# Head preparation under the input projection, a regrouped order of the modulation sums and fillers, and a second expert-choice layer on 32 live rows with nine landing places

## What is computed

```python
# first block
h = rms_norm(x, attn_norm_g);  proj = h @ w_in              # 1024 -> 3688 columns
dq, dk, dv, iq, ik, iw, cq, ckv, kpe, gd, gm = split(proj)  # 512 64 64 512 64 8 256 128 32 1024 1024
q_a, k_a = rope(rms_norm(dq heads)), rope(rms_norm(dk))     # 9 heads of 64: "qk"
q_i, k_i = rope(iq heads), rope(ik)                         # 9 heads of 64: "ix"
score = sum_h relu(q_i . k_i) * iw ; keep the top 64 keys of each query
out_a = attention(q_a, k_a, dv, only the kept keys)
q_b, kv_b = rms_norm(cq) @ mla_w_uq, rms_norm(ckv) @ mla_w_ukv   # then head norm, rope, causal attention
x += (sigmoid(gd) * (out_a @ w_br_dsa) + sigmoid(gm) * (out_b @ w_br_mla)) @ w_out
x += memory_cross_attention(...);  x += hierarchical_moe(...)    # 16 experts, 2 of a group
# second block: two layers, each modulated by m = silu(c) @ ada_w + ada_b  (6 x 1024 columns)
x += g1 * ssd_mixer(...)        # layer 0;   layer 1: attention over latent and context tokens
x += g2 * moe_ec(...)           # both layers, expert choice:
def moe_ec(h, router_w, w1, w3, w2):
    cap = 2 * T // 16                                # 32 tokens for each of 16 experts
    gate, idx = top_k(softmax(h @ router_w).T, cap)
    xg = h[idx]
    y = (silu(xg @ w1) * (xg @ w3)) @ w2 * gate      # w1, w3, w2: 1024 x 1024 each
    return zeros.at[idx].add(y)
return rmsnorm(x, final_norm_w)
```

## Time and profile before

| | us |
|---|---|
| median of 3 runs | 2287.35 (2286.69 to 2291.01) |
| the profiled execution | 2282.53 |
| its span, first to last instruction | 2280.7 |
| TensorE busy | 2077.5 (91%) |
| VectorE busy | 955.1 (42%) |
| ScalarE busy | 637.1 (28%) |
| filler products, 212 records | 104.0 |
| weights of both expert-choice layers | 427 GB/s in most slices from 1140 on |

### The profile page before, as it was taken

One profiled execution on the slowest core, in us unless ns is written; L12 is line 12 of the kernel. 1 busy time (PEld: TensorE's weight loads), 2 busy tenths in 40 slices (PEclk: granted clock), 3 DMA queues, 4 the chain that ended last, 5 costly groups with the idle time before them and its releaser, 6 DMA issues. The chain is left out here.

```text
span 2280.7 us, 25273 instructions
## 1 busy us (share of the span) xinstructions
PE 2077.5 (91%) x10338; PEld 1120.2 (49%) x10338; DVE 955.1 (42%) x1595; ACT 637.1 (28%) x1264; POOL 69.5 (3%) x95
## 2 busy tenths in 40 slices
PE   6978898899999999999999998988898899988887
PEld 5744444444467888888643333322445433332222
DVE  4375523545588988893432222222357400000001
ACT  4222312211257766772221111100117110100000
POOL 0001000000000000000000000000020000000000
PEclk9989998999999999999999999999999999999999
DMA  8656156899623333332389999999820399999996
GB/s 307 214 216 235 42 183 252 345 390 387 241 77 93 112 111 130 111 111 73 130 343 428 427 428 428 427 427 428 323 99 1 148 416 426 426 426 427 427 427 293
DMA packets 145705, 623.59 MB, mean 273 GB/s; under 512 B 14995, under 2 KB 65686, under 8 KB 108598
## 3 DMA queue, kind: packets, MB, share of 16 engines
q1 hardware_dynamic: 140672, 601.65, 66.1%
q0 software_dynamic: 2352, 16.91, 1.9%
q10 hardware_dynamic: 2566, 3.41, 0.5%
HBM read 620.76 MB, written 1.18 MB: 273 GB/s over the span
## 5 line engine op out<-in xcount | busy, mean ns | idle before, releaser
L2798 PE MATMUL bank<-slots,xgTe 128*64 128x512 f32 x1648 | 370.9, 596 | 44.0 <-DMA slots<-in_moe_w 44.0
L2798 PEld LDWEIGHTS bank<-slots,xgTe 128*64 128x64 f32 x1648 | 116.4, 137 | 276.0 <-issue 215.0
L3007 DVE TENSOR_TENSOR actse<-sge,bank 128x512 f32<-128x512 f32 x32 | 22.0, 688 | 529.1 <-PE bank L2798 529.1
L2798 PE MATMUL bank<-slots,aTe 128*64 128x512 f32 x832 | 189.6, 597 | 19.1 <-issue 19.1
L511 PE MATMUL bank<-slots_r 128*128 128x512 f32 x512 | 200.0, 391 | 0.0
L2911 ACT ACTIVATE sge<-bank 128x512 f32<-128x512 f32 x32 | 19.1, 597 | 485.2 <-PE bank L2798 485.2
L510 PE MATMUL bank<-hT_r,slots_r 128*128 128x512 f32 x384 | 154.0, 401 | 0.0
L512 PE MATMUL bank<-slots_r 128*128 128x512 f32 x384 | 150.3, 391 | 0.0
L574 PE MATMUL bank<-slots,hT 128*128 128x512 f32 (+1 forms) x320 | 131.5, 572 | 1.6 <-DVE hT L551 0.7
L2798 PEld LDWEIGHTS bank<-slots,aTe 128*64 128x64 f32 x832 | 61.1, 136 | 126.7 <-issue 126.7
L506 PE MATMUL bank<-consts 128*128 128x512 f32 x212 | 104.0, 644 | 7.7 <-PEq L1954 3.4
(11 more groups left out here) (536 smaller groups left out, 3116.8 us busy)
## 6 DMA issues: line engine op xcount, KB each, us to landing
slots<-in_moe_w SPq DMA_DIRECT2D x155, 2048.0 KB, 29.5
extra0e<-in_moe_w SPq DMA_DIRECT2D x25, 2048.0 KB, 29.5
slots<-in_ada_w SPq DMA_DIRECT2D x24, 2048.0 KB, 10.1
slots<-in_ssd_in_w SPq DMA_DIRECT2D x48, 512.0 KB, 5.3
slots<-in_moe_w_gate SPq DMA_DIRECT2D x23, 1024.0 KB, 10.6
slots<-in_moe_w_up SPq DMA_DIRECT2D x23, 1024.0 KB, 12.6
slots<-in_moe_w_down SPq DMA_DIRECT2D x23, 1024.0 KB, 7.5
rowsB<-acum_rows POOLq DMA_DIRECT2D x16, 1024.0 KB, 5.8
```

Of the source, the lines that this page charges most:

```text
L2798: i = pe.matmul(bank[64 * n:64 * n + 64, :], lhsT(4 * h + k), wv[:, 0, n * 512:(n + 1) * 512], start=(h == 0 and k == 0), stop=(h == 1 and ...
L3007: dve.tensor_tensor(acts[:, :], sg[:, :], psum[1][:, :], ALU.mult).then_inc(a_ready, 1)
```

## The change

It has six parts. (1) rope of ix, the sum, the scale and rope of qk are issued by VectorE inside the input projection, after the splits of the chunks 3 to 6, with scratch space in the buffer C. (2) The c norm of MLA (squares, roots, scales) moves to the front of DSA; DSA keeps one ada group, which comes after the relevances, and its VectorE part stands in round 4 of the top-k. (3) MLA has both its ada groups after its products; a new group, `mix_ada`, is put in the merge block. The list of weight pieces follows that order. (4) Fillers: 106 become 45. (5) In the second expert-choice layer the padding is gone: 32 columns in `xgT`, and silu, gate and scale work on the two live groups of 32 partitions, in two instructions each; `acts` is set to zero once. (6) That layer's ring has nine places; the ninth is extra2 with columns 2048 to 4095 of hT, free once `quarters` has been computed.

```diff
@@ stream of weights
         ada_weights()
+        weights("mla", [...])
         ada_weights()
-        ada_weights()
-        weights("mla", [...])
         ada_weights()
         weights("br_dsa", ...); weights("br_mla", ...)
+        ada_weights()
...
-        moe2_weights(1, (4, 5, 0, 1, 2, 3, SLOTS + 1, SLOTS + 2))
+        moe2_weights(1, (4, 5, 0, 1, 2, 3, SLOTS + 1, SLOTS + 2, SLOTS + 3))
@@ input projection, VectorE, after split_in(dve, n + 2, ...)
+                    if n == 3:
...
+                        rope(dve, link, ix, ix, tmp, 9, 32, 64, 0, cos(32), sin(32))
+                    if n == 4:
+                        hnorm.vector_sum(dve, link, qk, sq, 9, 64)
+                    if n == 5:
...
+                        hnorm.vector_scale(dve, link, qk, qk, [...], 9, 64)
+                    if n == 6:
+                        rope(dve, link, qk, qk, tmp, 9, 32, 64, 0, cos(32), sin(32))
@@ DSA, TensorE
-                ada0.tensor(pe)
-                pe.wait_ge(ix_ready, 1)
                 to_ixT.tensor(pe)
...
-                ada1.tensor(pe)
-                pe.wait_ge(qk_ready, 1)
+                ada0.tensor(pe)
                 to_qkT.tensor(pe)
-                hold(pe, 6)
                 to_qkT.wait_all(pe)
@@ DSA, VectorE, in the top-k
+                    if r == 4:
+                        ada0.vector(dve)
@@ MLA, TensorE
-                ada0.tensor(pe)
                 pe.wait_ge(c_normed, 1)
                 to_cT.tensor(pe)
...
+                ada0.tensor(pe)
                 ada1.tensor(pe)
-                hold(pe, 17)
                 pe.wait_ge(heads_ready, 1)
@@ merge
+                mix_ada.tensor(pe)
                 pe.wait_ge(merged_ready, 4)
                 to_mT.tensor(pe)
@@ memory block, SSD, attention
-                hold(pe, 3)
...
-                        hold(pe, 9, pair[0].ap)
+                        hold(pe, 8, pair[0].ap)
...
-                hold(pe, 5)
                 norm.tensor(pe)
-                hold(pe, 13)
...
-                hold(pe, 10)
+                hold(pe, 9)
@@ expert choice
-                    hold(pe, 7 if l == 0 else 4)
+                    if l == 1:
+                        hold(pe, 4)
                     norm.tensor(pe)
-                    hold(pe, 3 if l == 0 else 1)
...
+                    extra_room[2].freed = (bank_full, b.full)     # behind quarters
...
-                                    i = pe.matmul(bank[64 * n:64 * n + 64, :], lhsT(4 * h + k), ...
+                                    i = pe.matmul(bank[64 * n:64 * n + NJ * CAP, :], lhsT(4 * h + k), ...
...
+                LIVE = [slice(0, P)] if NJ == 2 else [slice(0, CAP), slice(64, 64 + CAP)]
...
-                        dve.memset(xgT[:, :, :, :, CAP:2 * CAP], 0.0)
+                        link(dve.memset(acts[:, :], 0.0))
...
-                        dve.tensor_tensor(acts[:, :], sg[:, :], psum[1][:, :], ALU.mult).then_inc(a_ready, 1)
+                        for r_ in LIVE:
+                            i = dve.tensor_tensor(acts[r_, :], sg[r_, :], psum[1][r_, :], ALU.mult)
+                        i.then_inc(a_ready, 1)
```

More of the change, by code:

```diff
@@ L212, in build @@
         banks = Banks(psum, emptied)
-        slot_loaded = [sem(f"slot_loaded{i}") for i in range(SLOTS + 3)]
+        slot_loaded = [sem(f"slot_loaded{i}") for i in range(SLOTS + 4)]
         ring = Ring(slots, slot_loaded)
@@ L262, in build @@
         ada_weights()
+        weights("mla", [(0, 2, 768, rows("mla_w_uq")), (1536, 1, 1024, rows("mla_w_ukv"))])
         ada_weights()
-        ada_weights()
-        weights("mla", [(0, 2, 768, rows("mla_w_uq")), (1536, 1, 1024, rows("mla_w_ukv"))])
         ada_weights()
@@ L317, in build @@
         w_v = [A[f"moe_w{m}_2"].rearrange("l e (h p j) n -> p (l e) h (j n)", h=2, j=4) for m in (1, 3, 2)]
-        extra_room = [Piece(None, None, 0, None) for _ in range(2)]
+        extra_room = [Piece(None, None, 0, None) for _ in range(3)]
         ring.last[SLOTS] = extra_room[0]
@@ L335, in build @@
         ring.last[SLOTS + 1] = ring.last[SLOTS + 2] = extra_room[1]
+        ring.last[SLOTS + 3] = extra_room[2]
         for n in (0, 1, 2):
@@ L910, in tensor @@
                         back(c - 1)
-                hold(pe, self.held)
                 back(self.pieces[-1])
@@ L1156, in _ @@
             def _(pool):
-                hnorm.pool(pool, 9, 64)
+                pool.wait_ge(c_squared, 4)
+                root(pool, 0, 2, MLA_QR)
+                root(pool, 2, 2, MLA_KVR, c_rooted)
             @block.scalar
             def _(act):
-                ada0.scalar(act)
+                for t in range(NT):
+                    act.activation(cn[:, t, 0:256], proj[:, t, O_CQ:O_CKV], ACT.Square,
+                                   accum_out=eps_rows[:, t:t + 1]).then_inc(c_squared, 1)
+                    act.activation(cn[:, t, 256:384], proj[:, t, O_CKV:O_KPE], ACT.Square,
+                                   accum_out=eps_rows[:, 2 + t:3 + t]).then_inc(c_squared, 1)
                 to_ixT.evacuate(act, ACTE)
@@ L1175, in _ @@
                 link = chain(dve, dve_step)
[L1176 to L1179 removed]
                 to_ixT.evacuate(dve, DVE)
[L1181 to L1183 removed]
+                dve.wait_ge(c_rooted, 1)
+                for t in range(NT):
+                    dve.tensor_scalar(cn[:, t, 0:256], proj[:, t, O_CQ:O_CKV], rstd[:, t:t + 1],
+                                      MLA_QR ** 0.5, ALU.mult, ALU.mult)
+                    i = dve.tensor_scalar(cn[:, t, 256:384], proj[:, t, O_CKV:O_KPE], rstd[:, 2 + t:3 + t],
+                                          float(MLA_KVR) ** 0.5, ALU.mult, ALU.mult)
+                i.then_inc(c_normed, 1)
                 for n, (t, h) in enumerate(pairs):
```

94 lines of the change are left out of this document (42 added, 52 removed).

## The result

The changed kernel takes 2255.4 us (2254.3 to 2259.3, four runs) against 2287.0 for the kernel before; the ratio is 0.987, with an interval of 0.9855 to 0.9885. A second comparison gave 0.988 (0.9862 to 0.9902). The forecast was 2256.9, in a range of 2247 to 2268. The total was right, and closer than its terms: two gains were forecast too small, by 3.6 and 2.4 us, and four were forecast too large, or a loss was missing, by 2.1 to 2.4 each. That these nearly cancel is luck.

A forecast was written before the change was run, and what follows sets the result against it. Engines wait at stage ends: a TensorE-VectorE chain bounds the stages in question before the second expert-choice layer, while both expert-choice layers stream weights. Terms sum to -30.5, taking the median 2287.35 to 2256.9 us; range 2247 to 2268.

The forecast's parts named there:

- The cover under the projection: Input projection: 16.5 us of VectorE head work fits between splits and copies, 3.6 us of room, at cost 0.
- DSA, -26.1 for -22.5: Sparse attention: attention starts at 140.6 instead of 164.17, -23.6, less 1 us for cold first items: -22.5 (-17 to -24).
- the 1 us given for a cold TensorE at the attention's start: DSA's attention: TensorE at half clock is slower than VectorE in the first items, costing 1 us.
- the other end of the range, -17: DSA: half clock also under the relevances, 14.3 us instead of 7.14, leaves a gain of only 17 us.
- MLA, -2.5 for -4.6: Latent attention: front -7.6, VectorE's own ada work +0.5, half clock on last transposes and first items +2.5: -4.6 (-7.1 to 0).
- Merge, +5.8 for +6.1: Merge block: mix_ada's 7.5 us, less a wait of 1.5 us for VectorE, stand in the open: +6.1.
- Memory block, +1.9 for -0.4: Memory block: its three fillers end 0.4 us after the VectorE copy they cover, so removing them gives -0.4.
- Expert choice 0, -3.6 for -1.2: First expert-choice layer's start: 2.5 us at full clock, but half-clock transposes 2.2 a tile, quarters and router some 2 more: -1.2.
- Expert choice 1, -3.0 for -5.4: Second expert-choice layer: ninth place -4.9, first release -1.6, doubled instructions at the end +1.1: -5.4 (-7 to +1).
- the clock takes it back: Rival: without 61 fillers, half clock holds in relevances, MLA items, SSD start and router; sum -14.7, 2272.6 us; chance 0.13.
- The ninth place is worth nothing: Rival, second expert-choice layer: its transfer queues or TensorE's head start only shifts; -5.4 becomes -0.5, 2261.8 us; chance 0.06.
- the second stream loses rate: Rival: second expert-choice layer's weight stream slows from 427 GB/s; at 390 GB/s the kernel takes 2296.9 us; chance 0.03.

The follow-up runs named there:

- the last two versions: Changed kernel, both free sum groups in DSA, loads reordered, one 96-partition instruction in expert choice 1: 2249.5 us; the same plus nine MLA fillers: 2246.8 us, both against the kernel before.
- the move into DSA: Changed kernel with the merge block's group of modulation sums moved into the sparse attention, compared with the kernel before: 2254.2 us (0.9865).

## Why the prediction was right, and where its terms were off

**The cover under the projection** held as reckoned: room 8.5 us where the prediction had 8.6, cost 0.

**DSA, -26.1 for -22.5.** The steps to the attention's start were right to 0.7 us. The term that failed is the 1 us given for a cold TensorE at the attention's start: the stage gained 2.3 there, because half clock at the start is cheaper than half clock in the middle, where the kernel before had it. That the drop fell there is luck as far as the runs show: the last two versions have the same DSA and their drop in different places. In the other end of the range, -17, the relevances would have run cold; they took 7.14, at full clock.

**MLA, -2.5 for -4.6.** Its front went as said, 7.4 us shorter. The head transposes and the items after them, partly cold, cost 2.9 for the 2.5 reckoned (1.7 and 1.2); the step that failed is that the products were taken at full clock: 10.56 for 8.86, 1.7 more. TensorE was busy 2.79 of 4 us from 156 to 160, 2.29 of 4 from 160 to 164 and 1.18 of 2 from 164 to 166, all at full clock, and then fell to 0.57 (166 to 170). The Trainium skill, "TensorE: Matmul & The Clock Gate", section on HAM oscillation, says that an engine with pauses starts the next stage cold; here the trace agrees in kind (granted clock 0.85 over the stage against 0.98), and the price was 4.6 us of this stage. Over the thirteen profiles this loss and DSA's gain go together: wherever DSA's attention took 23.6 to 23.8 us, MLA's products took 10.55, and wherever it took 24.2 or more, 8.86.

**Merge, +5.8 for +6.1**, and the move into DSA shows that these 5.8 us need not have been in the open.

**Memory block, +1.9 for -0.4.** The three fillers were worth nothing; the output product ran at half clock in part (granted 0.72), 9.83 for 7.13. The kernel before had its drop in the block too, but earlier in it, on the transposes (3.08 for 1.94) and the attention's first products (7.16 for 3.69). The prediction had no term for such luck; with the same code in this block its length runs from 69.3 to 75.1 us over the kernels here.

**First expert layer, +2.3 for 0.** Not foreseen; the waits that hold it are shown above, their cause stays open.

**SSD, -2.5 as forecast**, by the start: 21.2 and 21.7 for 25.3 and 24.6; the rest of the stage is 1.8 and 0.2 longer.

**Expert choice 0, -3.6 for -1.2.** The router is 3.6 earlier. 2.8 of them are the transposes: reckoned at 2.2 us a tile, they kept up with VectorE's tiles, 1.6 apart, though the granted clock was 0.56 from 1108 to 1112, so that VectorE waited 0.42 us for them where it had waited 3.20. The other 0.8 are the router's product: with the filler ahead of it gone, it took its chunks as VectorE wrote them, beginning 1.1 us after VectorE's first. The steps that failed are both prices of half clock: the slow tiles, and the 2 us more for quarters and router. The clock was back at 1.00 while the product ran, and it took as long as VectorE's eight instructions beside it:

```profile
1114.08 3.70 DVE L480 TENSOR_SCALAR hT<-bank,ncol,modcol 128x256 f32<-128x256 f32 x8 [0.42 <-PE bank L458]
...
1115.22 3.82 PE L2735 MATMUL bank<-hT,actse 128*32 128x512 f32 x16 [0.42 <-DVE hT L480]
```

**Expert choice 1, -3.0 for -5.4.** Three terms. The stream is 3.1 us shorter for 4.9 in these two pairs of profiles, 4.0 over all that were taken. The way to the first halves is 1.1 shorter for 1.6, since another engine's work came to be last. The tail is 1.3 longer for 1.1; its step was right, and shows that the live rows lose more than they save.

Of the rivals, "the clock takes it back" held in kind, not in size: the granted clock fell from 0.981 to 0.975 and 0.971, and what it took in MLA and the memory block, 4.6 and some 2, was made up by DSA and expert choice 0, whose gains were forecast 3.6 and 2.4 too low. "The ninth place is worth nothing" and "the second stream loses rate" fell, the latter measured at 0.5 us.

## What to carry to other kernels

Work that waits at the start of a stage may fit in the idle time of its engine in the stage before, if each piece is shorter than the idle time plus the lead of what comes after it; split it over several gaps, since what is over the room of one gap is paid in full (18.8 us of work in a room of 8.5 stalled TensorE for 10.3). Before work is put into the open to make room elsewhere, look for a wait of its engine under somebody else's chain, and check that the loads it needs aren't queued behind a place that frees late. Of the fillers tested here, only those paid that ended before the wait that they fill and stood ahead of work that TensorE leads.

## What the runs showed of the hardware

TensorE's granted clock fell in DSA's attention, or just ahead of it, in all thirteen profiles, with fillers and without. Where the attention started at full clock and had the drop well inside (five of them), it took 26.1 to 26.7 us; where it was cold from its start, or from some 2 us after it, 23.6 to 24.3. Where a drop falls differs between kernels with the same code there, but hardly between two executions of one kernel: every stage up to the memory block agrees within 0.12 us. A VectorE instruction on 32, 96 or 128 partitions of 512 columns took 0.68 to 0.69 us each, so rows left out save nothing unless an instruction goes. The weight streams vary by up to 0.5% from one execution to the next (432.9 and 430.9 us for the same kernel).
